# SwiGLU weights of a decoder layer on one core: a third row pair of each gate and up group computed as seven products of sums

## What is computed

```python
hf = rms_norm(x, norm_ffn)
gate, up = jnp.split(hf @ w_gu, 2, axis=-1)      # hf 256x2048, w_gu 2048x11264
return x + (jax.nn.silu(gate) * up) @ w_down
```

## Time and profile before

| | |
|---|---|
| median of 3 runs | 1103.49 us (1103.11 to 1104.87) |
| the profiled execution | 1103.19 us, span 1101.5 us |
| PE busy | 1090.1 us, 99% of the span |
| DVE busy | 864.0 us, 78% |
| ACT busy | 580.9 us, 53% |
| DMA | 215.31 MB, mean 195 GB/s |
| granted TensorE clock | 0.998 |

### The profile page before, as it was taken

One profiled execution on the slowest core, in us unless ns is written; L12 is line 12 of the kernel. 1 busy time (PEld: TensorE's weight loads), 2 busy tenths in 40 slices (PEclk: granted clock), 3 DMA queues, 4 the chain that ended last, 5 costly groups with the idle time before them and its releaser, 6 DMA issues.

```text
span 1101.5 us, 13909 instructions
## 1 busy us (share of the span) xinstructions
PE 1090.1 (99%) x5101; PEld 906.9 (82%) x5101; DVE 864.0 (78%) x1061; ACT 580.9 (53%) x705; POOL 40.6 (4%) x68
## 2 busy tenths in 40 slices
PE   8999999999999999999999999999999999999997
PEld 7897889888888888888888888888888888888885
DVE  5556866688756557988988888889888899899896
ACT  5655545555445444545545545546455556546553
POOL 2600000000010000000000000000000000000000
PEclk9999999999999999999999999999999999999999
DMA  8765646465546575656657557566565766666663
GB/s 285 217 197 168 189 128 183 154 172 153 190 176 223 178 267 171 211 171 215 202 158 230 167 174 241 175 192 210 170 212 194 282 203 216 199 200 213 195 226 116
DMA packets 110941, 215.31 MB, mean 195 GB/s; under 512 B 6956, under 2 KB 11632, under 8 KB 110000
## 3 DMA queue, kind: packets, MB, share of 16 engines
q1 hardware_dynamic: 108976, 205.36, 59.2%
q0 software_dynamic: 1632, 8.96, 2.2%
q10 hardware_dynamic: 288, 0.39, 0.1%
HBM read 210.49 MB, written 4.19 MB: 195 GB/s over the span
## 4 chain that ended last, share of the span: by engine, by line
PE 96%; DVE 2%; DMA 1%; issue 1%; SPq 0%; ACT 0%; POOLq 0%; POOL 0%; ACTq 0%; DVEq 0%
PE acc L1693 11%; PE acc L1694 11%; PE acc L1695 11%; PE acc L1413 11%; PE acc L1414 11%; PE acc L1415 11%; PE acc L1758 5%; PE acc L1759 5%; PE acc L1760 5%; PE mx L1405 2%; PE mx L1693 2%; PE mx L1694 2%; PE mx L1695 2%; PE mx L1758 1%; PE mx L1759 1%; PE mx L1760 1%
## 5 line engine op out<-in xcount | busy, mean ns | idle before, releaser
L759 DVE TENSOR_TENSOR w_lo<-raw,w_hi 128x1024 fp32r<-128x1024 f32 (+2 forms) x144 | 166.7, 1169 | 117.8 <-ACT w_hi L454 117.0
L454 ACT ACTIVATE w_hi<-raw 128x1024 fp32r<-128x1024 f32 (+2 forms) x143 | 143.4, 1013 | 135.0 <-PE acc L1415 132.7
L648 ACT ACTIVATE w_hi<-raw 128x1024 fp32r<-128x1024 f32 (+1 forms) x160 | 158.4, 1005 | 94.4 <-PE acc L1695 86.7
L1693 PE MATMUL acc<-w_hi,hT_hi 128*128 128x512 f32 x520 | 203.3, 391 | 0.0
L1179 DVE TENSOR_TENSOR w_lo<-raw,w_hi 128x1024 fp32r<-128x1024 f32 (+1 forms) x160 | 180.5, 1154 | 29.0 <-ACT w_hi L648 27.2
L1694 PE MATMUL acc<-w_lo,hT_hi 128*128 128x512 f32 x520 | 202.4, 389 | 0.0
L1695 PE MATMUL acc<-w_hi,hT_lo 128*128 128x512 f32 x520 | 202.3, 389 | 0.0
L1413 PE MATMUL acc<-w_hi,hT_hi 128*128 128x512 f32 (+2 forms) x416 | 157.7, 379 | 0.0
L1415 PE MATMUL acc<-w_hi,hT_lo 128*128 128x512 f32 (+2 forms) x416 | 155.5, 374 | 0.0
L1414 PE MATMUL acc<-w_lo,hT_hi 128*128 128x512 f32 (+2 forms) x416 | 155.5, 374 | 0.0
L1695 PEld LDWEIGHTS acc<-w_hi,hT_lo 128*128 128x128 f32 x520 | 97.6, 188 | 20.5
(11 more groups left out here) (299 smaller groups left out, 1553.3 us busy)
## 6 DMA issues: line engine op xcount, KB each, us to landing
raw<-in_w_gu SPq DMA_DIRECT2D x176, 512.0 KB, 4.2
raw<-in_w_down SPq DMA_DIRECT2D x88, 512.0 KB, 4.5
raw<-in_w_in SPq DMA_DIRECT2D x79, 512.0 KB, 3.9
raw<-in_w_out SPq DMA_DIRECT2D x32, 512.0 KB, 4.3
raw<-in_w_in SPq DMA_DIRECT2D x8, 272.0 KB, 2.8
raw<-in_w_in SPq DMA_DIRECT2D x8, 264.0 KB, 2.8
x<-in_x POOLq DMA_DIRECT2D x2, 1024.0 KB, 8.0
x_kept<-x POOLq DMA_DIRECT2D x2, 1024.0 KB, 6.1
```

The costliest lines, as they stand in the source:

```text
L648: act.activation(w_hi[:, v % R, c0:UC * GW], raw[:, i % R, c0:UC * GW], ACT.Copy).then_inc(hi_ready, 1)
L759: dve.tensor_tensor(w_lo[:, slot, 0:UC * width], raw[:, slot, 0:UC * width], w_hi[:, slot, 0:UC * width].bitcast(F32), ALU.subtract).then_ ...
L1693: pe.matmul(o, a[0], w[0], start=first, stop=False)
```

## The change

Row pairs 0, 1 and 2 of each group are sevens instead of 0 and 1. A group has 22 slots: 0 to 2 are gate 3 to 5, 3 to 6 seven 0, 7 and 8 gate 6 and 7, 9 to 12 seven 1, 13 and 14 up 3 and 4, 15 to 18 seven 2, 19 to 21 up 5 to 7. As 22 is no multiple of 4, the loops run two groups an iteration (`lin`, `ring`). The load numbers no longer follow the order of use: slot 2 uses load 4, seven 0 loads 2 and 3, slot 7 load 5, slot 8 load 8, seven 1 loads 6 and 7, slot 13 load 9, slot 14 load 12, seven 2 loads 10 and 11, slots 19 to 21 loads 13 to 15; SP issues them by number. ACT computes Silu of the gate directly, which takes DVE's `gated` away, and makes one 128x128 copy that DVE made. `act_low` and `act_sums` are one piece that stands behind seven 0's weight sums; `fold_gate` stands before slot 20's low part, `fold_up` after slot 21's. Once, in the first group, DVE makes the sums of the activations' third row pair (`third_summands`).

```diff
-FF_ORDER = [("gate", 2, 0, 0), ("gate", 3, 1, 1), ("gate", 4, 2, 2), ("gate", 5, 3, 3), ("seven", 0, 4, 4),
-            ("gate", 6, 6, 8), ("gate", 7, 7, 9), ("seven", 1, 8, 10)] + [("up", k, 8 + k, 12 + k) for k in range(2, UPG)]
-FF_SLOTS = 20
+FF_SUMMED = 3
+FF_ORDER = [("gate", 3, 0, 0), ("gate", 4, 1, 1), ("gate", 5, 4, 2), ("seven", 0, 2, 3), ("gate", 6, 5, 7), ("gate", 7, 8, 8),
+            ("seven", 1, 6, 9), ("up", 3, 9, 13), ("up", 4, 12, 14), ("seven", 2, 10, 15)] \
+    + [("up", k, 8 + k, 14 + k) for k in range(5, UPG)]
+FF_SLOTS = 22
 FF_BASE = U_FF + 2 * UPG - FF_SLOTS
-FF_SLOT_OF = [-4, -3, -2, -1] + [v + d for kind, _k, _i, v in FF_ORDER for d in ((0, 1) if kind == "seven" else (0,))]
+SEVEN_END = {k: v + 4 for kind, k, _i, v in FF_ORDER if kind == "seven"}
+FF_SLOT_OF = {i - R: i - R for i in range(R)}
+for _kind, _k, _i, _v in FF_ORDER:
+    FF_SLOT_OF[_i] = _v
+    if _kind == "seven":
+        FF_SLOT_OF[_i + 1] = _v + 1
...
+def lin(j, m, c=0):
+    p, o = j
+    return o * m + c if p is None else p * (2 * m) + (o * m + c)
+
+
+def ring(j, v):
+    return (v + 2 * ((j[1] - 1) % 2)) % R
...
             def load_ff(j, k, i, up):
-                sp.wait_ge(lo_ready, j * FF_SLOTS + (FF_BASE + FF_SLOT_OF[i] + 1))
+                freed = FF_SLOT_OF[12] - FF_SLOTS if i == 0 and j > 1 else FF_SLOT_OF[i - R]
+                sp.wait_ge(lo_ready, j * FF_SLOTS + (FF_BASE + freed + 1))
...
             for j in range(1, NG_FF):
-                for kind, k, i, _v in FF_ORDER:
+                for kind, k, i, _v in sorted(FF_ORDER, key=lambda entry: entry[2]):
...
                 for b in range(NB):
-                    act.activation(gate_s[:, b, :], acc[:, b, :], ACT.Tanh, scale=half_rs_h[:, b:b + 1])\
-                       .then_inc(sem("gate_tanh"), 1)
...
+                    act.activation(gate_s[:, b, :], acc[:, b, :], ACT.Silu, scale=rs_h[:, b:b + 1])\
+                       .then_inc(sem("gate_used"), 1)
...
+                if kept is not None:
+                    act.activation(actT_lo32[:, bass.ds(kept, 1), P:2 * P].rearrange("p c t -> p (c t)"), mx[:, 0, P:2 * P],
+                                   ACT.Copy).then_inc(sem("a21_kept"), 1)
...
-                    if kind == "up" and k == 4:
-                        act.wait_ge(unit_used, j * FF_SLOTS + (FF_BASE + 12))
-                        act.wait_ge(lo_ready, j * FF_SLOTS + (FF_BASE + 13))
+                    if kind == "up" and k == 7:
+                        act.wait_ge(unit_used, lin(j, FF_SLOTS, FF_BASE + SEVEN_END[2]))
+                        act.wait_ge(lo_ready, lin(j, FF_SLOTS, FF_BASE + SEVEN_END[2]))
                         act.activation(ff_sum[:, 0, 0, :], mx[:, 2, :], ACT.Copy).then_inc(sem("p1_kept"), 1)
...
                     if kind == "gate" and k == 5:
-                        act_high(j, j * 4 - 4)
-                    if kind == "up" and k == 6:
-                        act.wait_ge(sem("gate_folded"), j * 2)
-                        gate_tanh(j * FF_SLOTS + (FF_BASE + 14), j * 2)
+                        act_high(lin(j, 1), lin(j, 4, -4), lin(j, 4, -4) if summed else None)
+                act.wait_ge(sem("gate_folded"), lin(j, 2))
+                gate_silu(lin(j, FF_SLOTS, FF_BASE + SEVEN_END[2]), lin(j, 2))
...
-            def gated(tanhs):
-
-                for b in range(NB):
-                    dve.wait_ge(sem("gate_tanh"), tanhs + b + 1)
-                    dve.scalar_tensor_tensor(out=gate_s[:, b, :], in0=gate_s[:, b, :], scalar=1.0, in1=acc[:, b, :],
-                                             op0=ALU.add, op1=ALU.mult).then_inc(sem("gate_used"), 1)
...
+                dve.wait_ge(sem("act_hi"), lin(j, 1))
+                dve.wait_ge(sem("a21_kept"), lin(j, 1))
+                d = bass.ds(lin(j, 4, -3), 3)
+                dve.tensor_tensor(actT_lo[:, d, :].rearrange("p c t -> p (c t)"),
+                                  mx[:, 0:2, :].rearrange("p k n -> p (k n)")[:, T:4 * T],
+                                  actT_hi[:, d, :].rearrange("p c t -> p (c t)").bitcast(F32), ALU.subtract)\
+                   .then_inc(sem("act_lo_made"), 1)
+                c = bass.ds(lin(j, 4, -4), 1)
+                dve.tensor_tensor(actT_lo[:, c, 0:P].rearrange("p c t -> p (c t)"), mx[:, 0, 0:P],
+                                  actT_hi[:, c, 0:P].rearrange("p c t -> p (c t)").bitcast(F32), ALU.subtract)\
+                   .then_inc(sem("act_lo_made"), 1)
+                a11, a12_, a22_ = (mx[:, 0, c * P:(c + 1) * P] for c in (0, 2, 3))
                 s1, s3 = (s_32[:, g, i, :].rearrange("p g n -> p (g n)") for i in range(2))
-                c = bass.ds(j * 4 - 4, 1)
                 s2, s4 = (t[:, c, P:2 * P].rearrange("p c t -> p (c t)") for t in (actT_hi32, actT_lo32))
-                dve.wait_ge(sem("act_lo_made"), j)
-                dve.tensor_copy(s4, a21_).then_inc(sem("a21_kept"), 1)
-                dve.wait_ge(sem("a21_kept"), j)
...
+            def third_summands():
+
+                full = actT_lo32[:, FC - 2:FC, :]
+                a11, a21_, a12_, a22_ = (full[:, c, b * P:(b + 1) * P] for c in range(2) for b in range(NB))
+                s1, s3, s2, s4 = (third_32[:, i // 2, (i % 2) * P:(i % 2 + 1) * P] for i in range(4))
+                step(dve.tensor_tensor(full.rearrange("p c t -> p (c t)"),
+                                       hT_hi[:, 4:6, :].rearrange("p c t -> p (c t)").bitcast(F32),
+                                       hT_lo[:, 4:6, :].rearrange("p c t -> p (c t)").bitcast(F32), ALU.add))
+                settle()
+                dve.tensor_tensor(s1, a21_, a22_, ALU.add).then_inc(sem("ff_sums_made"), 1)
+                dve.tensor_tensor(s3, a11, a21_, ALU.subtract).then_inc(sem("ff_sums_made"), 1)
+                dve.wait_ge(sem("ff_sums_made"), 5)
+                dve.tensor_tensor(s2, s1, a11, ALU.subtract).then_inc(sem("ff_sums_made"), 1)
+                dve.wait_ge(sem("ff_sums_made"), 7)
+                dve.tensor_tensor(s4, a12_, s2, ALU.subtract).then_inc(sem("ff_sums_made"), 1)
...
             def fold_gate(j):
 
-                dve.wait_ge(unit_used, j * FF_SLOTS + (FF_BASE + 14))
-                dve.wait_ge(sem("p1_kept"), j)
+                dve.wait_ge(unit_used, lin(j, FF_SLOTS, FF_BASE + SEVEN_END[2]))
+                dve.wait_ge(sem("p1_kept"), lin(j, 1))
...
                 for kind, k, i, v in FF_ORDER:
                     if kind == "seven":
                         ff_weight_sums(j, i, k, opening)
+                        if k == 0 and summed:
+                            act_sums(j, bass.ds(lin(j, 1, -1), 1))
+                        elif k == 0:
+                            act_low(lin(j, 1), lin(j, 4, -4))
+                    if kind == "up" and k == 6:
+                        fold_gate(j)
                     ff_low(j, i, v)
                     if kind == "seven":
                         ff_low(j, i + 1, v + 1, GW)
@@ -1238,24 +1288,16 @@
                         if opening:
                             activate(FF_SLOTS + FF_BASE, 2)
                         else:
-                            activate_folded(j - 1, j * FF_SLOTS + FF_BASE)
-                    if kind == "gate" and k == 5:
-                        act_low(j, j * 4 - 4, summed)
-                        if summed:
-                            act_sums(j, bass.ds(j - 1, 1))
-                    if kind == "up":
-                        if k == 5:
-                            fold_gate(j)
-                        if k == 6:
-                            fold_up(j)
-                        if k == 7:
-                            gated(j * 2)
+                            activate_folded(lin(j, 1, -1), lin(j, FF_SLOTS, FF_BASE))
+                    if kind == "up" and k == 7:
+                        fold_up(j)
 
             first_gate_up()
-            gate_up(1, True)
-            with dve.Fori(2, SUMMED + 1) as j:
-                gate_up(j)
-            gate_up(SUMMED + 1, summed=False)
+            gate_up((None, 1), True)
+            with dve.Fori(1, NG_FF // 2) as p:
+                gate_up((p, 0))
+                gate_up((p, 1))
+            gate_up((None, NG_FF - 1), summed=False)
...
+                if k < 2:
+                    s1, s3, s2, s4 = ((ff_hi[:, k, i, :], ff_lo[:, k, i, :]) for i in range(4))
+                else:
+                    s1, s3, s2, s4 = (tuple(t[:, i // 2, (i % 2) * P:(i % 2 + 1) * P] for t in (third_hi, third_lo))
+                                      for i in range(4))
...
+                first, last = k == 0, k == FF_SUMMED - 1
```

More of the change, by code:

```diff
@@ L247, in summands @@
                     (s_hi[:, g0:g1, 3, :], a21(actT_lo, g0, g1), a21(actT_lo32, g0, g1)))
+        third_hi, third_lo, third_32 = (t[:, FC - 4:FC - 2, :] for t in (actT_hi, actT_lo, actT_lo32))
         def gl_u(b):
@@ L431, in _ @@
             pool.wait_ge(sem("gate_used"), 2 * NG_FF)
+            pool.wait_ge(sem("up_folded"), 2 * (NG_FF - 1))
```

(42 more changed lines are left out.)

89 lines of the change are left out of this document (46 added, 43 removed).

## The result

The changed kernel takes 1178.15 us in the median of four runs (1176.75 to 1182.71), against 1103.3 for the kernel before: 1.068 times its time, 95% interval 1.065 to 1.071. The forecast was 1157 us with a range of 1115 to 1172: the side is right, and the time lies 6 us outside the range. The profiled execution has a span of 1175.8 us, 74.3 more than before. PE is busy 94% of it (before 99%), DVE 76%, ACT 51%; the mean granted clock is 0.989.

The account below looks back on a forecast made before the run. PE was taken as the bound, DVE close behind; six waits of 6.45 us less 0.93 saved add 5.52 a group, 55.2 over ten, less 1.6: 53.6 on 1103.49 gives 1157 us, range 1115 to 1172.

Parts of the forecast that it names:

- Wait a: Slot 20: DVE's gate fold stands ahead of its low part, so PE waits 1.87 us a group.
- Wait b: Slot 3: load 4 and DVE's sums make its low part late; PE waits 0.82 us, about nothing in first and tenth groups.
- Waits c and e: Slots 8 and 14: loads 8 and 12 queue behind two others and land late; PE waits 0.86 us at each.
- Waits d and f: Slots 9 and 15: DVE makes the preceding late low part, then weight sums; PE waits 1.02 us at each.
- The sum: All six waits, 6.45 us a group, less 0.93 saved by fewer matmuls: a group goes from 43.34 to 48.86.
- the case's own bounds: Low and high values of waits a, b and c: 1140 to 1173 us, the upper end taken as 1168.
- Loads in time: Rival: loads land soon enough, only the waits at slots 20 and 3 stay; 1119 us, chance 0.12.
- No wait at all: Rival: PE keeps its pace throughout and the three saved matmuls a group show; 1094 us, chance 0.10.
- Table loads inside the groups: Rival: ACT loads a table before and after each Silu pair, 1.5 us a group more; 1172 us, chance 0.08.

Follow-up runs that it names:

- the last kernel: Changed kernel with loads 8 and 12 issued earlier, folds and Silu moved past each group's end (tenth included), activation sums behind slot 4's low part: 1097.17 us.

## Why the prediction was right on the side and wrong on the size

- **The mechanisms** were right. All six waits stand at the slots named, on the engine named, and no other of size. The runs tie four to the order of the loads (with it put right they are gone and the other two stay), one to the fold's place (its price appeared alone in the kernel before) and slot 3's to slot 0's low part. What failed is the size of terms in the sum: b above all, then c and e, then a.
- **Wait a, slot 20:** 1.87 forecast, 2.10 measured. The copy and the start of the fold took 0.10 more, the restart 0.11.
- **Wait b, slot 3:** 0.82 forecast, 1.49 measured. This is the step that failed most. I took load 4's landing at 3.6 us, from a single row. Here it took 4.4, and 4.4 to 4.7 in seven of the nine groups from the second on. The page's own list of loads had a median of 4.2 for w_gu before (4.4 after): a single low row was taken where the middle of many was at hand. In the two groups with a landing of 3.7 the wait is 0.76 and 0.82, so load 4's place behind slot 0's low part and the rest of this walk were right. (The restart added 0.11, and the activation sums took 2.01 instead of 2.15.)
- **Waits c and e, slots 8 and 14:** 0.86 forecast each, 1.42 and 1.15 measured. The third load in a row took 5.5 and 5.2 us, not 4.8. The low parts came 7.50 and 7.76 behind those of slots 10 and 4 in place of 7.2, and the restart adds 0.11.
- **Waits d and f:** 1.02 forecast, 0.98 and 0.99 measured. They needed only DVE's lengths, which were the rows' own; and the restart at the slot ahead, which makes PE 0.11 later, cancels their own.
- **The sum:** 6.45 forecast, 8.13 measured in this group, so 1.7 a group and 17 us in all. The 1.6 us that I took off for the first and tenth groups aren't seen in the total, though slot 3 has no wait in either, as I had said: the tenth has the wait of 2.42 at slot 14 instead and takes 51.69.
- **The range:** its upper end came from saying that the high ends of the terms hardly meet. They are not independent: slow landings sit in b, c and e, and the restart, which no term had, in a, b, c and e. By the case's own bounds the top was 1173, still short of 1178: a and b lie above their upper bounds (2.10 against 2.0, 1.49 against 1.3).
- **The rivals.** Loads in time (1119) is not what happened; its price is near the kernel with the loads put right, 1128.7, where a and b are left. No wait at all: no run of this order did it. Table loads inside the groups: there are none. I had misread the profile here: it has five loads before, not two in all, and Silu brings a sixth, once, at 410.8. By the Trainium skill ("ScalarE: Activation LUTs", "Table sets: the hidden batching unit") cheap functions such as copy are in every set, so that one extra load was to be expected, and the trace agrees: one more load, and none between copies and Silu from 412 to 931.

What stays open is why a load takes 3.7 us in one group and 4.4 to 4.7 at the same place in another: load 4 goes out 2.33 us behind the load before it at 580.01 and at 731.81 alike. No run was made on it. Also open is how much of the last kernel's two waits (0.80 and 1.12) at the change of stage is the reload of x beside w_down's loads.

## What to carry to other kernels

Before fewer matmuls are bought with more vector work, walk one period slot by slot: DVE's 40.0 us fit in 42.4, and it was still late at six hand-overs of a group. When the order of use of a ring of buffers changes, the order of issue has to follow it, since a load that is free to go waits behind the ones ahead of it in its queue. Put work that waits for the end of a sequence behind everything that is due sooner, check what it then pushes on the far side of the loop's edge, and price a load's landing by the middle of many rows with others in flight, not by the fastest.

## What the runs showed that I had not expected

**A wait costs its restart.** After each wait on a low part the second matmul of PE starts about 0.34 us behind the first instead of 0.23 (627.21 and 627.55 above; in the kernel before, 572.77 and 573.10). It is as much behind a wait of 0.4 as behind one of 2.2. Why is open.

**The clock fell behind some of the longest waits, and in the group shown it cost nothing.** Behind this wait at slot 20 PE's steps grow to 0.43 us (628.13, 628.56, 628.99 above). The stretches show the granted clock, third column from the end:

```profile
626.00:628.00 2.00, 0.79 (x3) 0.69 (x4) 2.00 (x3) 1.94 (x3) 0.00 (x0) 0.97 0.00 0
628.00:630.00 2.00, 2.00 (x6) 1.52 (x6) 2.00 (x4) 1.22 (x2) 0.00 (x0) 0.50 0.79 239
630.00:632.00 2.00, 2.00 (x8) 1.60 (x7) 1.75 (x2) 0.00 (x0) 0.00 (x0) 0.68 1.01 295
632.00:634.00 2.00, 2.00 (x11) 1.65 (x10) 0.69 (x1) 0.00 (x0) 0.00 (x0) 1.00 0.80 287
```

It is 0.50 in 628 to 630, the 1.2 GHz level, and 1.00 again from 632 on; PE had been busy 0.79 of the 2 us before. There are six such spells in the groups (from about 628, 679, 829, 881, 918 and 932), and the mean clock of 0.989 against 0.998 means some 20 us more at that level over the execution than before. Five of them stand behind slot 20 and one behind slot 14's wait of 2.42; behind the same 2.24 at slot 20 in the other five groups the clock stays full, so the length of the wait alone does not decide it. The Trainium skill ("TensorE: Matmul & The Clock Gate", Part 1) has these two levels and an engine that falls to the lower one when idle; the trace agrees on the levels, and on idle time ahead of each fall. Yet the group with the fall at 628 is no longer: from slot 20 to slot 20 it takes 677.84 - 627.21 = 50.63 us, the group before it, with the clock full, 50.64. The spell cost PE about 1.4 us, and the wait at slot 3 shrank from 1.63 to 0.21 instead. The group with the fall at 679 takes 50.53. While PE has waits ahead that another engine's chain sets, a slower PE only eats into them. For the falls at 829, 881 and 918 this isn't shown, since slot 14 waits longer in those two groups as well, and the one at 932 comes behind the last of the ten.
